# Sixteen-column products ahead of three groups of projections, and the last products of a network in two halves

## What is computed

```python
for l in range(DEPTH):   # DEPTH = 2
    h = h + hybrid_mixer(rms_norm(h, mix_norm_g[l]), w_in[l], ...)
    h = h + memory_cross_attention(rms_norm(h, xattn_norm_g[l]), ...)
    h = h + conv_ffn(rms_norm(h, ffn_norm_g[l]), w_up[l], conv_w[l], conv_b[l], w_down[l])
return rms_norm(h, final_norm_g)
```

## Time and profile before

| what | us |
|---|---|
| median of 3 runs | 842.92 |
| lowest and highest run | 842.56, 843.38 |
| the profiled execution, its own time | 842.58 |
| its span in the trace | 840.8 |
| PE busy | 830.2 (99%) |
| PEld busy | 773.4 (92%) |
| DVE busy | 612.3 (73%) |
| ACT busy | 493.7 (59%) |

### The profile page before, as it was taken

One profiled execution on the slowest core, in us unless ns is written; L12 is line 12 of the kernel. 1 busy time (PEld: TensorE's weight loads), 2 busy tenths in 40 slices (PEclk: granted clock), 3 DMA queues, 4 the chain that ended last, 5 costly groups with the idle time before them and its releaser, 6 DMA issues.

```text
span 840.8 us, 15177 instructions
## 1 busy us (share of the span) xinstructions
PE 830.2 (99%) x6413; PEld 773.4 (92%) x6413; DVE 612.3 (73%) x850; ACT 493.7 (59%) x693; POOL 19.4 (2%) x39
## 2 busy tenths in 40 slices
PE   8999999999999999999999999999999999999997
PEld 7999998889899999999999999888998999999996
DVE  5898977779667566556577988887776776667665
ACT  7955765577665454444568647745765654454534
POOL 5000001000000000000000000010000000000000
PEclk9999999999999999999999999999999999999999
DMA  9777654544437555565446555436516455565551
GB/s 327 239 136 224 228 183 152 200 138 164 150 104 248 200 201 182 178 205 187 151 146 237 151 172 184 179 130 233 175 68 201 149 200 201 186 215 169 182 175 51
DMA packets 112973, 151.40 MB, mean 180 GB/s; under 512 B 3785, under 2 KB 92809, under 8 KB 112905
## 3 DMA queue, kind: packets, MB, share of 16 engines
q1 hardware_dynamic: 112760, 150.16, 53.5%
q10 hardware_dynamic: 144, 0.26, 0.1%
HBM read 147.92 MB, written 1.18 MB: 177 GB/s over the span
## 4 chain that ended last, share of the span: by engine, by line
PE 96%; DVE 1%; ACT 1%; DMA 1%; issue 0%; SPq 0%; ACTq 0%
PE bank L755 26%; PE bank L756 25%; PE bank L757 25%; PE bank L837 5%; PE bank L880 3%; PE bank L964 2%; PE bank L1166 1%; PE bank L1144 1%; PE bank L902 1%; PE bank L977 1%; DMA raw<-in_w_few 1%; PE bank L821 1%; PE bank L1151 0%; PE bank L1099 0%; PE bank L1114 0%; PE bank L1012 0%
## 5 line engine op out<-in xcount | busy, mean ns | idle before, releaser
L1647 DVE TENSOR_TENSOR wlo<-raw,whi 128x2048 fp32r<-128x2048 f32 (+3 forms) x140 | 298.6, 2138 | 96.2 <-ACT whi L1256 95.2
L1256 ACT ACTIVATE whi<-raw 128x2048 fp32r<-128x2048 f32 (+3 forms) x144 | 257.2, 1789 | 49.9 <-PE bank L757 39.2
L755 PE MATMUL bank<-yhi,whi 128*128 128x256 f32 x688 | 190.6, 277 | 0.0
L756 PE MATMUL bank<-ylo,whi 128*128 128x256 f32 x688 | 190.3, 277 | 0.0
L757 PE MATMUL bank<-yhi,wlo 128*128 128x256 f32 x688 | 190.3, 277 | 0.0
L756 PEld LDWEIGHTS bank<-ylo,whi 128*128 128x128 f32 x688 | 129.4, 188 | 0.8
L755 PEld LDWEIGHTS bank<-yhi,whi 128*128 128x128 f32 x688 | 129.2, 188 | 0.9
L757 PEld LDWEIGHTS bank<-yhi,wlo 128*128 128x128 f32 x688 | 129.2, 188 | 0.0
L755 PE MATMUL bank<-whi,xhi 128*128 128x512 f32 (+2 forms) x256 | 90.2, 352 | 0.3 <-issue 0.3
L757 PE MATMUL bank<-whi,xlo 128*128 128x512 f32 (+2 forms) x256 | 88.5, 346 | 0.0
L756 PE MATMUL bank<-wlo,xhi 128*128 128x512 f32 (+2 forms) x256 | 88.4, 346 | 0.0
(11 more groups left out here) (317 smaller groups left out, 1389.1 us busy)
## 6 DMA issues: line engine op xcount, KB each, us to landing
raw<-in_w_up SPq DMA_DIRECT2D x44, 1024.0 KB, 5.0
raw<-in_w_down SPq DMA_DIRECT2D x22, 1024.0 KB, 4.8
raw<-in_w_in SPq DMA_DIRECT2D x10, 1024.0 KB, 5.0
raw<-in_w_xk SPq DMA_DIRECT2D x8, 1024.0 KB, 5.4
raw<-in_w_xv SPq DMA_DIRECT2D x8, 1024.0 KB, 4.9
raw<-in_w_out SPq DMA_DIRECT2D x8, 1024.0 KB, 5.0
raw<-in_w_xq SPq DMA_DIRECT2D x8, 1024.0 KB, 5.2
raw<-in_w_xo SPq DMA_DIRECT2D x8, 1024.0 KB, 4.9
```

Source lines behind the costliest of these rows:

```text
L755: mm(o, s_hi, m_hi, start=first, stop=False, skip_group_check=True)
L756: mm(o, s_hi, m_lo, start=False, stop=False, skip_group_check=True)
L1256: A(weight(whi, gu), raw[:, gu % RING, 0:SIZE[gu]], ACT.Copy).then_inc(hi_done, 1)
L1647: tt(weight(wlo, gu), raw[:, gu % RING, 0:SIZE[gu]], weight(whi, gu), ALU.subtract).then_inc(lo_done, 1)
```

## The change

Ahead of each layer's `first_units`, a product of 16 columns is issued, behind the wait for the first `xhi` block. `fg0` of the last layer is called with `stepped=True`, too. In the last layer bank 5 becomes `fd_3a`, which takes what `fd_3` took, but for the last group: there the 512 columns are made in two halves of 256 columns, the first half accumulated into `fd_3a`, the second into a fresh bank (`fd_3`, bank 0). PE signals after each half. DVE adds the whole of `fd_3a` to `h`, then does the scaling that stood in L2118, then adds the 256 columns of `fd_3`. ACT squares each half by itself, with one more small pass that joins the first half's sum to that of the row's other half.

```diff
     for i in (0, 2, 1, 3):
-        job(f"fd_{i}", 2 + i, f"fd{NP - 1}" if i == 3 else None)
+        if i == 3 and l + 1 == DEPTH:
+            job("fd_3a", 5)
+        job(f"fd_{i}", 0 if i == 3 and l + 1 == DEPTH else 2 + i, f"fd{NP - 1}" if i == 3 else None)
@@ first_units
                         hi_is(pe, l, "n1", k)
+                        if k == 0:
+                            mm(o_gq[:, 0:HALF], gq_hi[:, 0, :], xh[:, 0, 0:HALF], start=True, stop=True, skip_group_check=True)
                         mm(o_gq, gq_hi[:, k, :], xh[:, k, :], start=k == 0, stop=False, skip_group_check=True)
@@ last layer
-                            fm_unit("fg0", "n3")
+                            fm_unit("fg0", "n3", stepped=True)
@@ fd products
                             if g == 0:
-                                free(f"fd_{i}")
+                                free("fd_3a" if i == 3 and l + 1 == DEPTH else f"fd_{i}")
+                            if i == 3 and g == NP - 1 and l + 1 == DEPTH:
+                                free("fd_3")
+                                for half in range(2):
+                                    w = slice(512 + 256 * half, 768 + 256 * half)
+                                    for k in range(2):
+                                        last = split_mm(bank(("fd_3a", "fd_3")[half])[:, 0:256], fhi[:, g % 2, k, P:T], flo[:, g % 2, k, P:T],
+                                                        hi[:, k, w], lo[:, k, w], half == 1 and k == 0, k == 1)
+                                    last.then_inc(te_done, 1)
+                                continue
@@ scalar, at the end
-                    is_drained(act, DEPTH - 1, f"fd_{2 * n + t}")
-                    square(t, n, xv)
+                    if t and n:
+                        is_drained(act, DEPTH - 1, "fd_3a")
+                        link(A(xv[:, 1, 512:768], h[:, 1, 512:768], ACT.Square, accum_out=ss[:, 1, 1:2]))
+                        link(A(ss[:, 1, 0:1], ss[:, 1, 1:2], ACT.Identity, scale=1.0 / DM, bias=ss[:, 1, 0:1]))
+                        is_drained(act, DEPTH - 1, "fd_3")
+                        link(A(xv[:, 1, 768:1024], h[:, 1, 768:1024], ACT.Square, accum_out=ss[:, 1, 1:2]))
+                        A(rt[:, 1:2], ss[:, 1, 1:2], ACT.Sqrt, scale=1.0 / DM, bias=ss[:, 1, 0:1]).then_inc(rstd_ready, 1)
+                    else:
+                        is_drained(act, DEPTH - 1, f"fd_{2 * n + t}")
+                        square(t, n, xv)
@@ vector, at the end
+                    if i == 3 and l + 1 == DEPTH:
+                        is_filled(dve, l, "fd_3a")
+                        drain(tt(h[:, 1, 512:1024], h[:, 1, 512:1024], bank("fd_3a"), ALU.add))
+                        ts(tmb[:, 0, 512:1024], tmb[:, 0, 512:1024], rt[:, 0:1], None, ALU.mult).then_inc(fin_ready[0], 1)
+                        is_filled(dve, l, "fd_3")
+                        is_drained(dve, l, "fd_3a")
+                        drain(tt(h[:, 1, 768:1024], h[:, 1, 768:1024], bank("fd_3")[:, 0:256], ALU.add))
+                        continue
@@
-                    ts(tmb[:, 0, 512:1024], tmb[:, 0, 512:1024], rt[:, 0:1], None, ALU.mult).then_inc(fin_ready[0], 1)
                     with_gain(1, 0).then_inc(gained_ready, 1)
```

More of the change, by code:

```diff
@@ L262, in layer_drains @@
         v += [f"fa{p}", f"fg{p}"]
-    v += [f"fd_{i}" for i in (0, 2, 1, 3)]
+    v += [f"fd_{i}" for i in (0, 2, 1)] + (["fd_3a"] if l + 1 == DEPTH else []) + ["fd_3"]
     return s, [(l, n) for n in v]
@@ L1211, in _ @@
                                 way = from_the_end if i == 3 and k == 1 else (lambda v: v)
-                                last = split_mm(way(bank(f"fd_{i}")), fhi[:, g % 2, k, s], flo[:, g % 2, k, s],
+                                last = split_mm(way(bank("fd_3a" if i == 3 and l + 1 == DEPTH else f"fd_{i}")), fhi[:, g % 2, k, s], flo[:, g % 2, k, s],
                                                 way(hi[:, k, n * 512:(n + 1) * 512]), way(lo[:, k, n * 512:(n + 1) * 512]),
```

## The result

The changed kernel is slower by a little: 844.15 us median of 22 runs (842.98 to 845.39) against 842.91 of 22 for the kernel before, a ratio of 1.0015 with a 95% interval of 1.0008 to 1.0021. The forecast was 842.5 with a range up to 843.8. The profiled execution of after took 843.49 against 842.58 in before, and its span is 841.75 us, 0.92 longer than the 840.84 of before.

The account below looks back on a forecast made before the run. PE, busy 99% of the span, was taken as the bound, with steps bringing a faster pace. Terms -0.53 - 0.41 + 0 + 0.53 = -0.41 us on the median 842.92 gave 842.5, range 841.4 to 843.8.

Parts of the forecast that it names:

- The last layer's gate unit: Last layer's `fg0`: 144 products take 16.41 instead of 17.04 us (-0.63), the step costs 0.10; term -0.53 us.
- Layer 1's first units: Layer 1's row of 120 products turns fast (-0.53), the step costs 0.11; net term -0.41 us.
- Rival 1: Layer 1's step, landing in a running slow row, doesn't change the pace: +0.11 in all, 843.0 us; chance 0.20.
- Layer 0's first units: Layer 0's 120 products: gain and cost alike are absorbed by PE's wait for DVE's own chain; term 0.
- the wait at this kernel's L968: Layer 0, PE's wait for DVE (L964 before): forecast to grow to about 0.6 instead of 0.2 us.
- The end: Tail in halves: DVE adds 512, scales, adds 256; ACT late with its joining pass, root later; term +0.53 us.
- left for others: Remaining chance of 0.02 for other causes, such as a later row of 96 products turning, 0.42 us either way.
- Rival 2: Neither the last layer's nor layer 1's step changes the pace: +0.74, 843.7 us, slower than before; chance 0.14.

Follow-up runs that it names:

- reversed heads: Kernel before with 10 warm-ups, no steps, first feature block of both `fa0`, both `fg0` and both first units run from last column to first: 0.9989.
- after with 10 warm-ups: The changed kernel with 10 instead of 12 warm-up products at its beginning, against the kernel before: ratio 1.0009 (1.0000 to 1.0018).
- every head reversed: Kernel before with 10 warm-ups, no steps, columns reversed in the first feature block of every unit of 256-column products: 0.9997 (0.9988 to 1.0006).

## Why the prediction was wrong, point by point

The forecast was 0.41 us less, and the traces show 0.92 more. The step that failed is that a 16-column product ahead of a row brings the fast pace. It priced two terms: layer 1's, which came out at +0.11 instead of -0.41, and the last layer's, which came out in this trace by luck: in two of three traces it would have been +0.11. Beside it the sum lacked a term, the stop, +0.42. Two smaller ones, +0.19 and +0.15, stand below.

- *The last layer's gate unit, -0.53.* The row came out at 16.43 in the trace of after, and the step at 0.11 (660.08 to 660.19) instead of 0.10. But the step that the prediction took for the cause is not: the same step gave 17.05 in two of three executions. The failing step of the argument is "a row of products keeps the one it began with. What differs at the beginning: ... the 16-column product stands in front". The two paces and the 0.63 between them were right: 16.41 to 16.44 or 17.04 to 17.05 in every trace but one; which of them a row gets, one pair of stretches from one execution could not show. Layer 0's `fg0` with its step of 16 was fast in six executions of nine and slow in three.
- *Layer 1's first units, -0.41.* Rival 1 came out: +0.11. With a step the row was slow in three traces of three (and with one of 64 columns), without one in six of six. Rival 1 leaned on this step landing in a running slow row. That this is the reason is not shown: the last `fg0`'s step lands in a running row, too, behind the passes of `row`, and that row was fast once.
- *Layer 0's first units, 0.* The 120 products stayed slow, so there was no gain to absorb, and the wait at this kernel's L968 was not 0.6 but gone. That was a wrong sign of a right mechanism: the row behind them, `qk1` and `qk2`, had turned slow as well (0.4), PE was 0.50 late at 61 us (61.66 against 61.16), and the wait and the short stops behind it took up most of that: 0.15 was left at 66.9 us. In the kernel with the first units' steps alone PE waited there 1.8.
- *The end, +0.53.* Right: 0.52 and 0.53 in the two traces that have it, by the very order that was worked out (scaling, add of 512, scaling, add of 256; ACT late with its joining pass). DVE's three starts and ACT's four, counted from the scaling, are all within 0.02 of the forecast.
- *What was missing.* The stop at 549, +0.42 in after by its count; the sum put it at nothing. Its row stood in the trace of before, 0.26 of "issue" on PE, the only one on PE itself of more than 0.1. I had looked for who waits for whom, and this wait names nobody. An added product has two costs: its own place, and what it moves ahead of the next piece of instructions.
- *A later row turning*, a kind of thing that the prediction had among the 2 in 100 "left for others": the last layer's `fa0` was slow in after, +0.19 (5.54 to 5.73 us). None of the edits is shown to be its cause: it was slow in two of the traces with reversed heads, too, and fast in after with 10 warm-ups.

The sum of the parts, behind 181 us: step 0.11 and stop 0.42 make 0.53 of the second stretch's 0.54; step 0.11, `fg0` -0.61, `fa0` +0.19 and the end +0.53 make 0.22 in the third. With the 0.15 of layer 0 it is 0.90, where the span shows 0.92. The median of 22 runs, +1.24, lies between this and the sum with a slow `fg0`, 0.90 + 0.61 = 1.5; how often the row is slow in those 22 is not known, as only one of them has a trace. Rival 2 named this side, and its +0.74 was short by what it didn't know of, the stop.

The Trainium skill's rule of two read ports ("TensorE: Matmul & The Clock Gate", "Step-by-step: what each phase is for") says that loading the next weights takes no read bandwidth from the running product. That a row then has one pace was the prediction's conclusion, and no trace here bears it out: the same 144 products have two paces at a granted clock of 1.00, and between them there is only 16.49, in the kernel with every head reversed. The other conclusion from it, that a step can only cost, is nearer to what the runs showed than my terms were.

## What to carry to other kernels

A difference in pace between two stretches of one trace is a lead and not a cause: before an edit is priced by it, look at the same stretch in further executions. Here layer 0's `fg0`, with the same code, showed 16.41 to 16.43 in six of nine and 17.04 in three. Count what an edit adds to an engine's instruction stream, and look for "issue" stops on the engine that bounds the kernel: the one here sat at a fixed count, and four passes fewer ahead of it, in a place where the engine waits anyway, took it away (0.53 us). And where rows of equal products have two paces, try the column direction at the row's beginning, row by row: what turns one row fast can turn another slow.

## What the runs showed of the hardware that I had not expected

- Products of 128x256 with a new weight each follow one another at 0.113 or 0.118 us at the same granted clock. A row without a reversal inside it keeps its pace over a hundred products and more. Behind a wait the pace is thrown anew in each execution (layer 0's first 120 without a step: fast in three traces, slow in three); in other places it never changed (layer 1's first units, slow in all ten traces without reversed columns).
- Products with their columns reversed at its head turned a slow row fast in 16 of 17 cases in five rows that were slow in all traces without a step or reversal (the last `fg0` 5 of 5, layer 0's `fa0` 4 of 4, layer 1's first 48 products 4 of 4, its `qk0` 2 of 2, its `qk1` 1 of 2). It is no rule for all rows: in the one kernel with every head reversed `nk`'s two rows, as slow in all traces, stayed slow, and four rows that were fast in all other traces turned slow. Why the direction matters, no run here shows.
- PE stops when its 4368 products are done, at a fixed count, for 0 to 1.42 us, by how many are ahead. This one of the 51 pieces comes after 475 to 537 products and weight loads, where the median is some 250. Why it is late is open. From 543.0 to 544.8 us in before 140 short products stand ahead of it, 0.011 to 0.013 us apart, which use up instructions faster; that was not tried.
- The first 181 us, where DVE and ACT work off their own chain, took 181.4 to 184.2 us in the traces, whatever the edit. So two traces of a kernel are better compared behind that point.
